# A gated delta rule in 64 x 64 chunk blocks, with its solve issued in a staggered order

## The reference, cut to what matters

```
decay = where(i >= j, exp(g_i - g_j), 0)            # cumulative gates within a chunk
m     = where(i > j, (beta k) k^T * decay, 0)       # 64 x 64 for each chunk and head
u, w  = solve(I + m, [beta v, beta k exp(g)])       # unit lower triangular
a_qk  = q k^T * decay
for each chunk:                                     # the state loop
    v_new = u - w @ state
    o     = (q exp(g)) @ state + a_qk @ v_new
    state = state * exp(g_last) + (k exp(g_last - g))^T @ v_new
```

## Time and profile before

| | |
|---|---|
| median of 3 runs | 2844.61 us (2837.52 to 2846.0) |
| the profiled execution: its own time | 2846.07 us |
| its span | 2844.3 us |
| mean granted TensorE clock | 0.979 |
| PE, DVE, ACT busy in the span | 94%, 68%, 54% |

### The profile page before, as it was taken

One profiled execution on the slowest core, in us unless ns is written; L12 is line 12 of the kernel. 1 busy time (PEld: TensorE's weight loads), 2 busy tenths in 40 slices (PEclk: granted clock), 3 DMA queues, 4 the chain that ended last, 5 costly groups with the idle time before them and its releaser, 6 DMA issues.

```text
span 2844.3 us, 42630 instructions
## 1 busy us (share of the span) xinstructions
PE 2685.4 (94%) x15459; PEld 2262.1 (80%) x15459; DVE 1921.4 (68%) x2167; ACT 1543.6 (54%) x1580; POOL 180.8 (6%) x209
## 2 busy tenths in 40 slices
PE   5999998999999999989999999999999999999997
PEld 3666887777777777768897987799897979877996
DVE  3444667999999999975686465645456874656554
ACT  3333546878888787854555443444335564534342
POOL 0000010000000000000082000000000820000000
PEclk9999998999999999999999999999999999999999
DMA  7344538999999999954343015444543430154444
GB/s 272 131 166 183 194 118 337 392 385 385 388 379 389 385 390 380 392 224 173 124 162 136 1 67 205 180 178 159 190 154 143 149 142 7 68 192 186 158 174 185
DMA packets 80079, 613.23 MB, mean 216 GB/s; under 512 B 16053, under 2 KB 21749, under 8 KB 24889
## 3 DMA queue, kind: packets, MB, share of 16 engines
q1 hardware_dynamic: 79928, 611.18, 56.2%
HBM read 610.10 MB, written 1.05 MB: 215 GB/s over the span
## 4 chain that ended last, share of the span: by engine, by line
issue 46%; PE 34%; DVE 8%; POOL 5%; ACT 4%; DMA 2%; POOLq 0%; DVEq 0%; ACTq 0%; SPq 0%
PE psum_scalar L1771 5%; PE psum_scalar L1772 5%; DVE weight_slabs_rounded L1730 3%; PE psum_vector L548 3%; PE psum_vector L550 2%; PE psum_vector L549 2%; POOL arena L3393 2%; PE psum_scalar L575 2%; ACT arena_rounded L1719 2%; PE psum_scalar L548 2%; PE psum_vector L1744 2%; PE psum_scalar L549 2%; PE psum_scalar L550 2%; POOL arena L3396 2%; DMA weight_slabs<-in_mixer_slabs 1%
## 5 line engine op out<-in xcount | busy, mean ns | idle before, releaser
L2143 DVE TENSOR_TENSOR weight_slabs_rounded<-weight_slabs,arena_rounded 128x2048 fp32r<-128x2048 f32 x208 | 477.8, 2307 | 366.8 <-ACT arena_rounded L2140 306.9
L2140 ACT ACTIVATE arena_rounded<-weight_slabs 128x2048 fp32r<-128x2048 f32 x208 | 396.1, 1913 | 395.4 <-PE psum_vector L550 236.7
L548 PE MATMUL psum_scalar<-arena_rounded,arena_rounded 128*128 128x256 f32 (+1 forms) x1456 | 474.7, 326 | 29.0 <-DVE weight_slabs_rounded L2143 15.2
L548 PE MATMUL psum_vector<-arena_rounded,arena_rounded 128*128 128x512 f32 (+3 forms) x1264 | 458.8, 363 | 20.2 <-DVE weight_slabs_rounded L2143 20.1
L1730 DVE TENSOR_TENSOR weight_slabs_rounded<-weight_slabs,arena_rounded 128x2048 fp32r<-128x2048 f32 x195 | 437.8, 2287 | 19.1 <-ACT arena_rounded L1719 11.2
L1719 ACT ACTIVATE arena_rounded<-weight_slabs 128x2048 fp32r<-128x2048 f32 x195 | 367.9, 1910 | 52.7 <-PE psum_scalar L1772 23.1
L550 PE MATMUL psum_vector<-arena_rounded,arena_rounded 128*128 128x512 f32 (+1 forms) x896 | 349.9, 391 | 0.0
L549 PE MATMUL psum_vector<-weight_slabs_rounded,arena_rounded 128*128 128x512 f32 x880 | 345.5, 393 | 0.0
L548 PEld LDWEIGHTS psum_scalar<-arena_rounded,arena_rounded 128*128 128x128 f32 x1456 | 280.7, 193 | 62.2 <-issue 24.7
L1771 PE MATMUL psum_scalar<-arena_rounded,arena_rounded 128*128 128x512 f32 x768 | 310.3, 404 | 19.8 <-DVE weight_slabs_rounded L1730 12.0
L548 PEld LDWEIGHTS psum_vector<-arena_rounded,arena_rounded 128*128 128x128 f32 (+2 forms) x1264 | 238.7, 189 | 62.4 <-DVE weight_slabs_rounded L2143 26.5
(11 more groups left out here) (487 smaller groups left out, 4414.8 us busy)
## 6 DMA issues: line engine op xcount, KB each, us to landing
weight_slabs<-in_layer_slabs SPq DMA_DIRECT2D x103, 2048.0 KB, 7.8
weight_slabs<-in_expert_slabs SPq DMA_DIRECT2D x195, 1024.0 KB, 8.0
arena<-in_expert_slabs SPq DMA_DIRECT2D x96, 1024.0 KB, 7.8
weight_slabs<-in_mixer_slabs SPq DMA_DIRECT2D x32, 2048.0 KB, 7.8
weight_slabs<-in_layer_slabs SPq DMA_DIRECT2D x6, 1024.0 KB, 5.5
arena<-in_mem SPq DMA_DIRECT2D x3, 1024.0 KB, 11.8
arena<-in_b_gate SPq DMA_DIRECT2D x6, 512.0 KB, 8.4
constants<-in_constants SPq DMA_DIRECT2D x1, 1043.5 KB, 9.5
```

What stands on the lines that cost most here:

```text
L548: pe.matmul(out, left[0], right[0], start=start, stop=False)
L2140: e.activation(fr(high), low, ACT.Copy).then_inc(S("weights_high"), 1)
L2143: e.tensor_tensor(fr(low), low, fr(high).bitcast(F32), ALU.subtract).then_inc(S("weights_split"), 1)
```

## The change

What it does:

- **Compact blocks.** m, a_qk, Dm, factor and the solve's DT are kept as 64 x 64 blocks a head, with the first chunk of a tile on partitions 0 to 63 and the second on 64 to 127. `four_blocks` makes a bank of 4 heads as 8 products of 64 x 64 x 64, alternating between the two chunks. The decays of 4 heads and both parts fit one A bank; so do those products of keys in a V bank, now 8 products of 64 output rows.
- **The solve.** Step 0's turn is a product with a folded identity; the turned matrix of the first step comes from a DVE mask (`solve_turned`). The turned inverse is its own product, factor times DT, in place of a transpose. The order is three factors, the first inverse, the fourth factor, the other inverses. The masks and copies are 256 columns a bank in place of 512. Step 5's result is spread to the 128 x 128 DT by two half copies a bank.
- **The state loop.** Heads 0 to 3 go to output partitions 0 to 63 and heads 4 to 7 to 64 to 127, in one bank, alternating. DVE and ACT copy half of vnew each. a_qk times vnew uses the chunk's 64 rows alone. PE waits for the state of all heads at once.
- **Moved.** Slab 21's rounding goes ahead of the solve on ACT and behind steps 2 and 3 on DVE, with its high parts in other places; the Silu of z is split in two behind the first two chunks' vnew copies.
- **Memory's rows** are squared at n = 1, normed at n = 2, and turned at n = 3 and 4, in V banks.

```diff
+                def four_blocks(ring, j, left, right, after=None):
+                    bank = ring.open(after)
+                    pe.sem_inc(S("blocks_seen_free"), 1)
+                    for g in range(4):
+                        for rows in CHUNKS:
+                            mm = pe.matmul(bank[rows, g * C:(g + 1) * C], left[rows, 4 * j + g, :], right[rows, 4 * j + g, :],
+                                           start=True, stop=True)
+                    ring.close(mm)
+                    return ring.n - 1
...
+                    for j in range(2):
+                        bank = A.open()
+                        pe.matmul(bank, ident_r, barrier.rearrange("p a n -> p (a n)").unsqueeze(1).broadcast_to([P, 4, P]),
+                                  start=True, stop=False)
+                        for g in range(4):
+                            for part, row in ((0, R_Q), (1, R_K)):
+                                for rows in CHUNKS:
+                                    at = g * P + part * C
+                                    mm = pe.matmul(bank[rows, at:at + C], logs[rows, t, row, 4 * j + g:4 * j + g + 1].broadcast_to([C, C]),
+                                                   ident[rows, rows], start=False, stop=g == 3 and part == 1)
+                        A.close(mm)
...
+                def factors_of(s, t, j):
+                    if s > 1:
+                        A.copied(inverse[t, j])
+                    else:
                         V.copied(new_factor[t, j])
+                    new_factor[t, j] = four_blocks(V, j, MA[t][:, :, 1, :], Dm[t])
+                def inverses_of(s, t, j):
+                    V.copied(new_factor[t, j])
+                    after = transposed.get((t, j))
+                    if s < 5:
+                        inverse[t, j] = four_blocks(A, j, DT_blocks[t], factor[t], after)
+                    transposed[t, j] = four_blocks(A, j, factor[t], DT_blocks[t], after)
+                for s in range(1, 6):
+                    for nth in range(3):
+                        factors_of(s, *PAIRS[nth])
+                    inverses_of(s, *PAIRS[0])
+                    factors_of(s, *PAIRS[3])
+                    for nth in range(1, 4):
+                        inverses_of(s, *PAIRS[nth])
...
+                HEADS = [(h, slice(h // 4 * C, h // 4 * C + C), slice(h % 4 * P, (h % 4 + 1) * P)) for g in range(4) for h in (g, 4 + g)]
...
+                    new_v = V.open()
+                    vnew_at = V.n - 1
+                    for h, side, cols in HEADS:
+                        pe.matmul(new_v[side, cols], DT[t][:, h, rows], vb[t][:, h, :], start=h % 4 == 0, stop=False)
...
+                    pe.wait_ge(S("state_ready"), 7 * l + 2 * c + 1)
...
+                    V.copied(vnew_at)
+                    pe.wait_ge(S("vnew_by_scalar"), 4 * l + c + 1)
...
+                    for h, side, cols in HEADS:
+                        mm = pe.matmul(out_bank[side, cols], MA[t][rows, h, 0, :], vnew[rows, h, :], start=False, stop=h % 4 == 3)
...
+                    if n == 3:
+                        pe.wait_ge(S("memn_ready"), l + 2)
+                        memory_to_T(0)
+                    if n == 4:
+                        memory_to_T(4)
...
-                step.go(e.memset(vnew, 0.0))
+                for t in range(NT):
+                    step.go(e.memset(DT[t], 0.0))
...
+                    step(tt(MA[t][:, :, 1, :], MA[t][:, :, 1, :], over(const("fold"), H2), ALU.add))
+                    step.go(tt(DT_blocks[t], MA[t][:, :, 1, :], over(const("solve_turned"), H2), ALU.mult))
...
+                    if s in (2, 3):
+                        weights.stop = FIRST[22]
+                        weights.upto(FIRST[21] + s - 2)
```

More of the change, by code:

```diff
@@ new lines, in pe_layers @@
+                    V.close(mm)
+                    out_bank = A.open()
+                    for h, side, cols in HEADS:
+                        pe.matmul(out_bank[side, cols], raw[:, h, in_T], st[:, h, :], start=h % 4 == 0, stop=False)
+                    V.copied(vnew_at)
+                    pe.wait_ge(S("vnew_by_scalar"), 4 * l + c + 1)
+                    if c < 3:
+                        for j in range(2):
+                            four(V, j, lambda b, h: pe.matmul(b, kdec[t][rows, h, :], vnew[rows, h, :], start=True, stop=True))
+                    else:
+                        pe.sem_inc(S("blocks_seen_free"), 1)
@@ L2636, in pe_layers, with memory_to_T @@
                             used_by(A)
+                def memory_to_T(first):
+                    for k in range(first, first + 4, 2):
+                        bank = V.open()
+                        for j in range(2):
+                            for t in range(NT):
+                                mm = pe.transpose(bank[:, (2 * j + t) * P:(2 * j + t + 1) * P],
+                                                  mem_rows[:, t, (k + j) * P:(k + j + 1) * P], ident)
+                        V.close(mm)
                 for n in range(6):
@@ L3175, in vec_layers @@
                 signal("norms_ready")
-                for i, cell in enumerate(barrier):
-                    step.go(ts(cell, const(("tri_f", "before")[i]), -NEG, NEG, ALU.mult, ALU.add))
+                for i, name in enumerate(("tri_f", "before")):
+                    for half in range(2):
+                        rows = slice(half * C, half * C + C)
+                        step.go(ts(barrier[rows, i, :], const(name)[rows, rows], -NEG, NEG, ALU.mult, ALU.add))
                 step.go(e.tensor_copy(ident_r, ident))
@@ L3225, in vec_layers @@
                 for s in range(6):
-                    mask = over(solve[:, s * P:(s + 1) * P], 4)
+                    mask = over(solve[:, s * C:(s + 1) * C], 4)
                     for t in range(NT):
@@ L3238, in vec_layers @@
                     t, rows = c // 2, slice(c % 2 * C, (c % 2 + 1) * C)
-                    for j in range(2):
-                        V.give(e.tensor_copy(vnew[rows, 4 * j:4 * j + 4, :], V.take()[rows, :].rearrange("p (h n) -> p h n", n=P)))
+                    V.give(e.tensor_copy(vnew[rows, 0:4, :], V.take()[0:C, :].rearrange("p (h n) -> p h n", n=P)))
                     if c < 3:
@@ L3322, in feed_forward_low, with memory_gains @@
                     e.sem_inc(S("ff_split"), 1)
+                def memory_gains(first):
+                    gains(e, step, [part[:, first:first + 4] for part in memT], V.take, V.give,
+                          lambda k: mem_gain[:, KC + first + k:KC + first + k + 1], 4)
                 for n in range(6):
```

216 lines of the change are left out of this document (83 added, 133 removed).

## The result

The changed kernel takes 2790.34 us (median of 4 runs, 2789.78 to 2799.2) where the kernel before, run beside it, takes 2844.32 (2837.52 to 2846.0). The ratio is 0.9822, with a 95% interval of 0.981 to 0.9833. In a later comparison it was 0.9823 (0.9808 to 0.9838). It is faster, by 54 us where 69 were forecast; 2790 lies within the range of 2762 to 2818, and just inside the upper end of the likeliest case's own range (2792).

What follows compares the result with a forecast made beforehand. PE alone was taken to bound the changed stage. Terms of 7.3 + 17.3 - 0.1 + 11.0 - 0.9 gave 34.6 us a layer, 69.2 for both, so 2776 after a profiled 2846.07; range 2762 to 2818.

Steps and rivals of the forecast that it cites:

- the likeliest case: Whole kernel: the forecast of 2776 us holds, with own range 2764 to 2792; chance 0.62.
- The front, 7.3: From stage start to the solve's first step: 7.3 us a layer saved, DVE setting when tile 1 is ready.
- The cost of a small record, 0.028: PE's 64 by 64 block products: 0.028 us a record as diagonal blocks overlap, 0.055 without overlap.
- rival (B): Block products: diagonal blocks of the array do not overlap; 6.5 us a layer saved, time 2832; chance 0.12.
- The solve, 17.3: Solve: 12 banks of 0.455 a step, PE staying the bound, 25.7 us for 43.1; 17.3 a layer saved.
- a step is record time and nothing else: Solve before the change: a step's 8.98 us is 80 PE records of 0.112, 8.96.
- A step over 7 makes me wrong: Sign in the new profile: a solve step, forecast at 5.5 us, refutes the forecast if longer than 7.
- Rival (C), PE not fed at that rate: Block products: records 0.040 us apart, 12.5 a layer lost, time 2800; chance 0.16 together with the increments.
- The increments: PE's semaphore increments ahead of 61 banks: taken as free; if each waits 0.2 us, 12.2 a layer, 2800.
- The state loop, 11.0: State loop: 5.85 us a chunk, PE and the copy chain about level, 22.6 for 33.6; 11.0 a layer saved.
- Memory's rows and the end, 0.9 lost: Gate stage and behind the loop: 0.4 us lost for memory's rows, 0.5 for later output copies, a layer.
- Rival (D), the clock: Changed stage: PE granted 1.2 GHz throughout, its terms double, time 2891; chance 0.06.

Runs made afterwards that it cites:

- the repeated one: The changed kernel unaltered, profiled once more beside the versions made from it: 2792.72 us, ratio to the kernel before 0.9823.
- two experiments: Each against the changed kernel: nine semaphore increments a bank in place of one, 2900.22 us; slab 21's rounding put back in the state loop, 2813.65 us.
- the first experiment: Changed kernel with four block products a bank (64 weight columns, 128 streamed) for eight of 64 by 64, altering what is computed: 2768.83 us, ratio to before 0.9736.

## Why the prediction was right, and where it was wrong

- **PE bounds the stage, and what is saved there reaches the end.** Right. The two stages gave 25.4 and 24.8 in the profiled run (25.8 and 27.3 in the repeated one), and ahead of, between and behind them the kernel is the same within 2.4 us.
- **The front, 7.3.** Right: 6.8 (first factor product 21.3 after the start, it was 28.1), DVE setting tile 1, ready at 20.35.
- **The cost of a small record, 0.028; rival (B).** Right: 0.029, diagonal blocks overlap in one bank. The rule quoted from the Trainium skill (TensorEngine Tiling (Array Packing), Restrictions and Gotchas) does not bind here as worded: row tiles at 0 and 64 wrote one bank in the same 0.03, each its own partitions.
- **The solve, 17.3.** Wrong: 8.0. The step that failed is "a step is record time and nothing else" carried over to records a quarter as far apart (0.029, where it was 0.112). I checked the bank of 0.455 against masks, copies and latency, and these did keep up; I did not check it against the instructions themselves. Before, a bank was 8 records, some 17 entries, in 0.90 of array time; now it is 16 records, 34 entries, in 0.47. So PE takes nearly four times as many entries in a microsecond, and their fetching, which the array's time hid, shows. The array's part was sized well (28.15 busy, seven record ends of 0.2 to 0.3 among it, for 25.7); the missing term is 6.9 of stops. "A step over 7 makes me wrong" came true at 7.5. That 2790 still lies in the likeliest case's own range is luck: that range was worked out from changes of shape, and not from a solve 9.3 a layer longer.
- **Rival (C), PE not fed at that rate.** This is what happened, in another shape: not 0.040 a record throughout but 0.029 with stops, which makes 35.05 / 896 = 0.039 on the mean. Its step of 7.7 was measured at 7.5, its 2800 at 2790, and it charged the front too, whose short runs had no stop. I gave it 0.16 together with the increments, mostly because four records had started within 0.02: a burst of four tells nothing of a rate over 900. The 62 ns a matmul that I cited from the Trainium skill (TensorE: Matmul & The Clock Gate, Wait — 56ns, not 53.3ns?) for decoding in microcode is not what happened: a product here is two matmuls in 0.058.
- **The increments.** Free at one a bank, as taken, but by a narrow margin (0.15 each in PE's sequencer).
- **The state loop, 11.0.** Right: 10.7, chunk 5.91 for 5.85, the last one 1.33 late for 1.0. What I booked as 0.3 for moving DVE's rounding out was the price before; in the shortened loop leaving both roundings there would have cost 11 to 12 a layer. The move is a condition of the gain, not an extra.
- **Memory's rows and the end, 0.9 lost.** The wait at 1950 keeps its end and grows from 2.42 to 3.37, as forecast; the 0.53 behind it is gone. From one stage's end to the start of the next layer's, the two profiled runs differ from before by 2.2 more and 0.5 less, so the small term itself can't be told.
- **Rival (D), the clock.** Not in the changed stage (1.00), where single stops of 1.44 did not lower it. But two experiments ran at 0.50: one stopping 0.4 behind every bank, one behind single waits of 2.1 and 3.3. And right behind the stage it fell for 3.4 us, a small cost that the prediction did not have: in the repeated profile behind the last chunk's wait of 1.33, in both layers, and in the first one behind the wait near 1693, which has grown from 1.25 to 1.87. Repeated, then first:

```profile
1646.40:1649.80 3.40, 3.40 (x9) 2.65 (x8) 2.27 (x2) 0.99 (x2) 0.00 (x0) 0.50 0.00 0
```

```profile
1673.80:1677.20 3.40, 3.40 (x9) 2.63 (x9) 3.09 (x4) 2.17 (x2) 0.00 (x0) 0.51 0.67 284
```

What stays open: why a transfer of instructions starts only 1.7 to 2.6 behind the last stop, and so why 256 entries last 4.3 to 5.2 us and not less.

## What to carry to other kernels

Count instructions beside array time. Here a block of 256 entries of PE's queue took 4.3 to 5.2 us to come; where the array finished one in 3.5, it stopped, where one lasted 6.3, it did not. What makes a block that short here is products of 64x64 in two passes, and merging or replacing such products pays though the array's work stays the same. When PE's part of a loop is cut, list everything else queued on the engines that feed it: work that was hidden now costs its length (5.4 us of waits here), and about as much again (some 6) where the wait lowers the clock.

## What was unexpected of the hardware

- The supply of instructions: blocks of 256 entries (16,384 bytes), 4.3 to 5.2 us a block over long runs of short records, with stops of 0.5 to 1.4 in the first layer; none where a block lasted longer (6.3), as in the first experiment (18 entries a bank, 0.444). The Trainium skill (Runtime: NRT & Kernel Launch, Instruction fetch mechanics) says that instructions come in 16 KiB blocks of 256 through a queue of the engine's own, and that fetching is mostly hidden behind the pace of dispatch. Size and queue agree with the trace (eight transfers of 16,384 bytes in the solve); that it is hidden agrees with the kernel before, which has no such stop in its solve, but not with this one: 6.9 us a solve.
- An increment alone in PE's queue costs 0.15, as much as five of the short records; PE hides it as long as it has products ahead.
- Records of neighbouring groups overlap across the border of a group if they lie on different column halves, so the order within a group matters less than it looks.
